# The gates of a hybrid mLSTM and attention layer as seven block products in place of eight, with an opening in another order

## What is computed

```python
mod = jax.nn.silu(c) @ w_ada[l] + b_ada[l]
shift, scale, gate = jnp.split(mod[:, None, :], 3, axis=-1)
h = rms_norm(x, g_norm[l]) * (1.0 + scale) + shift
proj = h @ w_in[l]
xa, va, oa, za, ia, fa, qa, ka, vat, zb, ga, gb = jnp.split(proj, split_at, axis=-1)
...
y_m = (h_m * jax.nn.silu(za)) @ w_out_mlstm[l]
...
y_a = (o_a * jax.nn.silu(zb)) @ w_out_attn[l]
merged = jax.nn.sigmoid(ga) * y_m + jax.nn.sigmoid(gb) * y_a
x = x + gate * (merged @ w_out[l])
return rms_norm(x, g_final)
```

## Time and profile before

| | us |
|---|---|
| median of 3 runs | 1460.41 |
| lowest, highest | 1460.26, 1461.08 |
| the profiled execution, its own time | 1462.57 |
| its span, first to last instruction | 1460.7 |
| TensorE busy | 1423.8 (97%) |
| VectorE busy | 764.3 (52%) |
| ScalarE busy | 485.3 (33%) |
| GpSimd busy | 368.1 (25%) |

### The profile page before, as it was taken

One profiled execution on the slowest core, in us unless ns is written; L12 is line 12 of the kernel. 1 busy time (PEld: TensorE's weight loads), 2 busy tenths in 40 slices (PEclk: granted clock), 3 DMA queues, 4 the chain that ended last, 5 costly groups with the idle time before them and its releaser, 6 DMA issues.

```text
span 1460.7 us, 18452 instructions
## 1 busy us (share of the span) xinstructions
PE 1423.8 (97%) x7465; PEld 1224.1 (84%) x7465; DVE 764.3 (52%) x1308; ACT 485.3 (33%) x859; POOL 368.1 (25%) x188
## 2 busy tenths in 40 slices
PE   3999999999999999999999999999999999999997
PEld 3698888889888888988888898888888888888885
DVE  6777566447466745635574554557373111112565
ACT  5666223443422353342335334323441000001122
POOL 3022111123111112211111221111154333443541
PEclk8999999999999999999999999999999999999998
DMA  6511111041221114211111421011172212124543
GB/s 258 186 58 53 39 35 39 30 145 60 100 65 45 44 36 150 83 31 43 30 29 30 145 73 44 30 30 43 31 279 82 65 65 66 65 65 152 155 135 111
DMA packets 51965, 117.79 MB, mean 81 GB/s; under 512 B 20769, under 2 KB 20897, under 8 KB 51877
## 3 DMA queue, kind: packets, MB, share of 16 engines
q1 hardware_dynamic: 47928, 104.01, 21.7%
q10 hardware_dynamic: 2832, 8.53, 1.9%
q0 software_dynamic: 1120, 4.06, 1.0%
HBM read 101.16 MB, written 15.43 MB: 80 GB/s over the span
## 4 chain that ended last, share of the span: by engine, by line
PE 92%; DVE 4%; DMA 3%; ACT 1%; issue 0%; SPq 0%; DVEq 0%; ACTq 0%
PE banks L464 26%; PE banks L463 26%; PE banks L462 26%; PE banks L747 2%; PE banks L737 2%; DMA x_rows<-in_x 2%; PE banks L698 2%; PE banks L704 2%; DVE y L1623 1%; PE banks L756 1%; PE banks L685 1%; PE banks L696 1%; PE banks L448 1%; PE banks L449 1%; PE banks L453 1%; PE banks L725 1%
## 5 line engine op out<-in xcount | busy, mean ns | idle before, releaser
L462 PE MATMUL banks<-h_hi,whi 128*128 128x512 f32 x1120 | 446.0, 398 | 0.0
L464 PE MATMUL banks<-h_hi,wlo 128*128 128x512 f32 x1120 | 437.4, 391 | 0.0
L463 PE MATMUL banks<-h_lo,whi 128*128 128x512 f32 x1120 | 436.5, 390 | 0.0
L602 POOL TENSOR_TENSOR wlo<-wraw,whi 128x1024 fp32r<-128x1024 f32 x75 | 192.0, 2560 | 842.4 <-ACT whi L827 842.4
L464 PEld LDWEIGHTS banks<-h_hi,wlo 128*128 128x128 f32 x1120 | 210.2, 188 | 44.6
L463 PEld LDWEIGHTS banks<-h_lo,whi 128*128 128x128 f32 x1120 | 210.6, 188 | 41.6
L462 PEld LDWEIGHTS banks<-h_hi,whi 128*128 128x128 f32 x1120 | 210.5, 188 | 41.1
L462 PE MATMUL banks<-whi,h_hi 128*128 128x256 f32 x480 | 135.8, 283 | 0.0
L464 PE MATMUL banks<-whi,h_lo 128*128 128x256 f32 x480 | 135.8, 283 | 0.0
L463 PE MATMUL banks<-wlo,h_hi 128*128 128x256 f32 x480 | 135.8, 283 | 0.0
L1471 DVE TENSOR_TENSOR num<-qa,banks 128x512 f32<-128x512 f32 x16 | 11.0, 688 | 184.6 <-PE banks L464 175.6
(11 more groups left out here) (271 smaller groups left out, 2248.0 us busy)
## 6 DMA issues: line engine op xcount, KB each, us to landing
wraw<-in_w_all SPq DMA_DIRECT2D x100, 512.0 KB, 3.5
s_wada<-in_w_ada_cols SPq DMA_DIRECT2D x16, 512.0 KB, 5.2
raw_lo<-in_x SPq DMA_DIRECT2D x8, 512.0 KB, 9.1
qm<-group_weights SPq DMA_DIRECT2D x8, 512.0 KB, 6.4
mlstm_branch<-xc SPq DMA_DIRECT2D x8, 512.0 KB, 8.7
part<-in_w_ada_gate SPq DMA_DIRECT2D x16, 256.0 KB, 3.4
b_raw<-mlstm_branch SPq DMA_DIRECT2D x8, 512.0 KB, 6.7
merged<-num ACTq DMA_DIRECT2D x8, 512.0 KB, 2.6
```

The source lines that it names most:

```text
L462: t_.matmul(out, w_hi, x_hi, start=first, stop=False)
L463: t_.matmul(out, w_hi, x_lo, start=False, stop=False)
L464: return t_.matmul(out, w_lo, x_hi, start=False, stop=last)
L602: nc.gpsimd.tensor_tensor(wlo[:, hi, :], wraw[:, q % 2, :], whi[:, hi, :].bitcast(F32), ALU.subtract).then_inc(w_split, 1)
```

## The change

**The gates.** The first pair of chunks (ga and gb of tile 0) is made as before, with the right half of the tokens first. The pairs 1 to 7 are made by seven products of blocks in place of eight. The weights of a pair are four quarters (ga or gb, first or second four row tiles) and h is four blocks (first or second four row tiles, left or right 512 tokens). Products 1 and 2 and 3 take a block of h as it is; products 5, 6, 7 and 4 take the sums t1, t2, t3 and t4 of blocks. Each product is 4 row tiles x 3 passes x 512 tokens. VectorE makes t1 ahead of `weigh_groups` of the last head, and t2, t3, t4 at the start of `merge`, in two pieces each of 128 x 1024; ScalarE copies their high parts and VectorE subtracts for the low parts. t3 is written over the h blocks that only the first pair reads. For each pair GpSimd makes four sums of quarters (`combine`, one of them in the new buffer `w_sum`) and seven low parts (`low`); ScalarE makes the seven high parts, in four places that go round (`weight_slot`). The results are put together by one copy on ScalarE (`keep_first`) and seven adds on VectorE (`plus`), each of one SBUF and one PSUM input, and the sigmoids are taken in place in SBUF and kept for all eight tiles.

**The order around them.** `merge_groups` of the last head moves behind the adds of pair 1. All branch products come after all gates. um and ua are loaded and split as the last pair ends, and w_out while the branches run, in rooms of their own. The softmax's exp of the last head (`group_exp`) is issued after the sigmoid of zb.

**The opening.** The first weight chunk is loaded ahead of x. VectorE squares tiles 0, 1, 6 and 7. GpSimd splits the second chunk only once the fifth tile is scaled. ScalarE keeps three transposed tiles before the second root.

**The closing.** TensorE waits for all three row vectors (48) in place of the gate's alone. Semaphores are merged in several places, and one counter of VectorE's steps serves all stages.

```diff
-BY_DVE = 2
+BY_DVE = (0, 1, 6, 7)
+BY_ACT = tuple(t for t in range(NCH) if t not in BY_DVE)
...
+        T["first_weights"](sp, 0)
         for t in range(NCH):
-            if t == NCH // 2:
-                T["first_weights"](sp, 0)
             sp.dma_start(x_raw[:, t, :], a["x"][t * P:(t + 1) * P, :]).then_inc(tile_in[t], 16)
...
         weights(0)
+        pool.wait_ge(x_norm, NCH // 2 + 1)
         weights(1)
...
+        A(xs[:, 2, 7:8], one[:], ACT.Abs_reciprocal_sqrt).then_inc(c_sig, 1)
+        act.wait_ge(c_sig, 3)
+        act.dma_start(m["szb"][0:ROPE, :].bitcast(I32), a["positions"].partition_broadcast(ROPE)).then_inc(pos_in, 16)
+        for t in BY_ACT:
             square(t)
-        root(0)
-        for t in range(NCH // 2, NCH - 1):
-            square(t)
-        keep_turned(0)
-        square(NCH - 1)
-        root(1)
-        act.dma_start(m["szb"][0:ROPE, :].bitcast(I32), a["positions"].partition_broadcast(ROPE)).then_inc(pos_in, 16)
-        for t in range(1, NCH):
+            if t == NCH // 2 - 1:
+                root(0)
+        for t in range(NCH):
+            if t == NCH // 2 - 1:
+                root(1)
             keep_turned(t)
...
+        for b in range(2):
+            for t in BY_DVE:
+                if t // 4 == b:
+                    square(t)
+            normalise(b)
...
             silu_za(1)
+            if i == HEADS - 1:
+                for q in range(2):
+                    ks = slice(2 * q, 2 * q + 2)
+                    t1 = T["sums"][1][2][:, ks, :]
+                    step(v.tensor_tensor(t1, h_hi[:, ks, HALF:].bitcast(F32), h_hi[:, ks, 0:HALF].bitcast(F32), ALU.subtract))
+                    step(v.tensor_tensor(t1, t1, h_lo[:, ks, HALF:].bitcast(F32), ALU.add))
+                    v.tensor_tensor(t1, t1, h_lo[:, ks, 0:HALF].bitcast(F32), ALU.subtract).then_inc(T["t_raw"], 1)
             weigh_groups()
             silu_zb()
-        merge_groups(HEADS - 1)
+        T["shared"]["merge_groups"] = merge_groups
...
+def products_of(p):
+
+    return (1, 5, 6, 2, 7, 4, 3) if p == 1 else (5, 4, 6, 7, 1, 3, 2) if p == KT - 1 else (5, 1, 2, 4, 6, 7, 3)
...
+    factors = {1: (h_hi[:, 0:KH, LEFT], h_lo[:, 0:KH, LEFT]), 2: (h_hi[:, KH:, LEFT], h_lo[:, KH:, LEFT]),
+               3: (h_hi[:, KH:, RIGHT], h_lo[:, KH:, RIGHT]), 4: (t4_hi[:], t4_lo[:]), 5: (t1_hi[:], t1_lo[:]),
+               6: (t2_hi[:], t2_lo[:]), 7: (t3_hi, t3_lo)}
+    sum_of = {5: 0, 6: 1, 7: 2, 4: 3}
+    quarter = {(r, c): raw[:, r, c * HALF:(c + 1) * HALF] for r in range(2) for c in range(2)}
+    spare = lambda p: mg if p == KT - 1 else sig[KT - 1][:, 1]
+    sums_of_weights = lambda p: {5: x_sum[:], 6: x_sum[:], 3: x_sum[:], 7: quarter[1, 0]} if p == 1 else \
+        {5: x_sum[:], 6: spare(p)[:, LEFT], 3: spare(p)[:, RIGHT], 7: x_sum[:]}
+    plain = {1: quarter[0, 0], 2: quarter[0, 1], 4: quarter[1, 1]}
+    source = lambda p, j: plain[j] if j in plain else sums_of_weights(p)[j]
+    made = lambda p, j: 4 * (p - 1) + ((5, 7, 6, 3) if p == 1 else (5, 6, 3, 7)).index(j) + 1
...
+        def load_pair(p):
+            for c in range(2):
+                sp.wait_ge(s_split, 1 + max(at_product(p - 1, j) for j in ((1, 2), (4, 7) if p == 2 else (4, 5))[c]))
+                sp.dma_start(raw[:, c, :], a["w_all"][Q0 + 2 * p + c]).then_inc(w_in[c], 16)
...
+        load_pair(2)
+        load_pair(3)
+        sp.wait_ge(T["ua_done"], HEADS + 1)
+        sp.dma_start(ua_d[HEADS - 1], T["mixing"]["szb"][:]).then_inc(ua_out, 16)
+        for p in range(4, KT):
+            load_pair(p)
...
+            if k % KH == 0:
+                sp.wait_ge(gprod, 1 + at_product(KT - 1, (5, 6)[k // KH]))
+            sp.dma_start(b_raw[k], um_d[k // 2, k % 2]).then_inc(tile_in[k], 16)
...
+        add, sub = ALU.add, ALU.subtract
+
+        def combine(out, x, y, op):
+            nc.gpsimd.tensor_tensor(out, x, y, op).then_inc(s_added, 1)
...
+            part = sums_of_weights(p)
+            if p > 1:
+                pool.wait_ge(s_split, PRODUCTS * (p - 1))
+            combine(part[5], quarter[1, 0], quarter[1, 1], add)
+            if p == 1:
+                pool.wait_ge(s_added, made(p, 5))
+                combine(part[7], quarter[0, 0], quarter[1, 0], sub)
+                low(1)
+                low(5)
+                after(5)
+                combine(part[6], part[5], quarter[0, 0], sub)
+                low(6)
+                after(6)
+                combine(part[3], quarter[0, 1], part[6], sub)
+                for j in (2, 7, 4, 3):
+                    low(j)
+            else:
+                low(5)
+                combine(part[6], part[5], quarter[0, 0], sub)
+                pool.wait_ge(s_added, made(p, 6))
+                combine(part[3], quarter[0, 1], part[6], sub)
+                after(5)
+                pool.wait_ge(s_added, made(p, 3))
+                combine(part[7], quarter[0, 0], quarter[1, 0], sub)
+                for j in products_of(p)[1:]:
+                    low(j)
+
+        for r in range(2 * KT):
+            n, to = width(r), (r + 1) % 2
+            pool.wait_ge(bw_high, r + 1)
+            nc.gpsimd.tensor_tensor(wlo[:, to, 0:n], raw[:, to, 0:n], whi[:, to, 0:n].bitcast(F32), sub).then_inc(bw_split, 1)
...
+        def product(p, j):
+            o = at_product(p, j)
+            bank_free(o)
+            to = bank(p, j)
+            pe.wait_ge(s_split, o + 1)
+            if p == 1 and j in sum_of:
+                pe.wait_ge(t_lo_done, 2 * sum_of[j] + 2)
+            hi, lo = factors[j]
+            at = weight_slot(o)
+            for k in range(KH):
+                cols = slice(k * P, (k + 1) * P)
+                mm = three_pass(t_, to, whi4[:, at, cols], wlo4[:, at, cols], hi[:, k, :], lo[:, k, :],
+                                k == 0, k == KH - 1)
+            mm.then_inc(gprod, 1)
...
+        for h in (1, 0):
             for j in range(2):
...
+                first_pair(j, h)
+        for p in range(1, KT):
+            for j in products_of(p):
+                product(p, j)
+        branch(um_at(0), 0, 0, KT, 0)
+        branch(um_at(1), 1, 0, KT, 0)
+        branch(ua_at(0), 0, KT, HEADS, 2)
+        branch(ua_at(1), 1, KT, HEADS, 2)
+        for m in range(2, KT):
+            branch(um_at(m), m, 0, KT, 0)
+            branch(ua_at(m), m, KT, HEADS, 2)
...
+        sum_high(1, t1_hi, t1_raw)
+        first_sigmoid(0, 1)
+        sum_high(2, t2_hi, t2_raw)
+        first_sigmoid(1, 1)
+        first_sigmoid(0, 0)
+        weight_high(1, 1)
+        weight_high(1, 5)
+        first_sigmoid(1, 0)
+        weight_high(1, 6)
+        weight_high(1, 2)
+        sum_high(3, t3_hi, t3_raw)
+        order_ = [(p, j) for p in range(1, KT) for j in products_of(p)]
+        for o in range(PRODUCTS * (KT - 2)):
+            p, j = order_[o]
+            if j == 1:
+                keep_first(p)
+            if o + 4 < len(order_) - 3:
+                weight_high(*order_[o + 4])
+            if o == 2:
+                sum_high(4, t4_hi, t4_raw)
+            if p > 1 and j == products_of(p)[1]:
+                sigmoids(p - 1)
...
+        weight_high(KT - 1, 1)
+        branch_high(0)
+        for k in range(2):
+            split_high(k)
+        weight_high(KT - 1, 3)
+        for k in range(2, 4):
+            split_high(k)
+        keep_first(KT - 1)
+        weight_high(KT - 1, 2)
+        for k in range(4, KT):
+            split_high(k)
+        branch_high(1)
+        sigmoids(KT - 1)
+        for k in range(KT, KB):
+            split_high(k)
+        branch_high(2)
...
+        def sum_raw(out, parts):
+
+            for q in range(2):
+                ks = slice(2 * q, 2 * q + 2)
+                t = out[:, ks, :]
+                (x, y, op), rest = parts[0], parts[1:]
+                ins = v.tensor_tensor(t, x[:, ks, :], y[:, ks, :], op)
+                for y, op in rest:
+                    step(ins)
+                    ins = v.tensor_tensor(t, t, y[:, ks, :], op)
+                ins.then_inc(t_raw, 1)
+
+        def sum_low(j, hi, lo, raw_):
+            for q in range(2):
+                ks = slice(2 * q, 2 * q + 2)
+                dve.wait_ge(t_hi_done, 2 * j - 2 + q + 1)
+                v.tensor_tensor(lo[:, ks, :], raw_[:, ks, :], f(hi[:, ks, :]), sub).then_inc(t_lo_done, 1)
+
+        def plus(p, name, out, x, j):
+
+            dve.wait_ge(gprod, 1 + at_product(p, j))
+            dve.wait_ge(part_added, added_part(p, name) - 1)
+            v.tensor_tensor(out, x, bank(p, j), add).then_inc(part_added, 1)
...
+        def merge_tile(m):
+
+            b0 = 4 * (m % 2)
+            if m == 0:
+                dve.wait_ge(s_split, PRODUCTS * (KT - 1))
+                dve.wait_ge(sig_done, 4 * KT)
...
+        dve.wait_ge(T["zb_done"], HEADS)
+        sum_raw(t2_raw, [(f(h_hi[:, KH:, RIGHT]), t1_raw, sub), (f(h_lo[:, KH:, RIGHT]), add)])
+        sum_low(1, t1_hi, t1_lo, t1_raw)
+        sum_low(2, t2_hi, t2_lo, t2_raw)
```

(40 more changed lines are left out.)

510 lines of the change are left out of this document (305 added, 205 removed).

## The result

The changed kernel takes **1468.68 us** (median of 5 runs, 1467.71 to 1469.03), the kernel before beside it 1460.41 (1459.85 to 1462.24). The ratio is 1.0053, 95% interval 1.0041 to 1.0064: slower by 6.0 to 9.4 us. I had forecast 1463.4 with a range up to 1468.0, so the time lies 0.7 us above the range. The kernel before has times of two kinds in the record of the first four experiments: 13 of its 23 executions took 1459.7 to 1461.3 us with a mean granted clock of 0.995 to 0.997, and ten took 1462.1 to 1463.1, nine of them with 0.992 or 0.993, as in the profiled execution (1462.57 us, 0.992).

What follows compares the result with a forecast made beforehand. PE, busy 97% of 1460.7 us, was taken to bound the kernel. Terms -19.0 - 1.2 + 0.4 + 19.1 + 2.6 + 1.1 = +3.0 us on the median 1460.41 gave 1463.4 us, eight-in-ten range 1446 to 1468.

Steps and rivals of the forecast that it cites:

- Term 1: Gates: 84 of 768 matmuls removed at 0.2267 us each, -19.0 us, all on PE.
- the 1405 that was named as a sign: Whole kernel, page of after: PE busy near 1405 us if the removal of matmuls holds.
- Term 2: Opening: Newton ends five us earlier, but blocked scalings and modulation sums leave -1.2 us, bounds -5.2 and 0.
- Term 3: First pair of gates, right half first: ScalarE's copy of its bank comes between, +0.4 us.
- Term 4: First new pair: VectorE's sums of h alternate with GpSimd; PE stalls 17.3 us, then half clock; +19.1 us.
- Later pairs: Gate pairs after the first new one: GpSimd's 14.3 us fit in PE's 19.0, costed at nothing.
- the third rival: Second new pair: GpSimd's low parts alternate with the merging and fall behind, +2 to +5 us more, 1467 us; chance 0.12.
- The prediction's own sign: Forecast is wrong if PE's waits in the first new pair sum under 8 us, or waits appear in later pairs.
- Term 5: Last pair and branches: two products wait 0.4 to 0.9 us each, um tiles 0 to 2; +2.6 us, bounds 0 and 5.
- Term 6: Closing: PE waits for all three rows, the last being gf, +1.1 us, bounds 0 and 1.5.
- The first rival: First new pair: sums of h hardly meet GpSimd, stall 3 to 7 us, total -12.2, 1448 us; chance 0.25.
- The second: Opening: gains its five us if modulation sums don't block on GpSimd, total about -0.8, 1459.6 us; no separate chance.

Runs made afterwards that it cites:

- e8: The changed kernel with ScalarE's second root ahead of the second to fourth copies of turned tiles: 1465.51 us, ratio 1.0029.
- e1: The kernel before with the changed kernel's new opening alone: 1462.63 us, ratio 1.0003.
- e5: The changed kernel with five useless matmuls between TensorE's last transposes and its first product: 1466.54 us, ratio 1.0035.
- e2: The changed kernel with GpSimd's low parts of the first new pair's weights covering 8 of 512 columns: 1461.71 us, ratio 1.0000.
- e9: e7 with the last szb sent after the fourth pair's weights and the last pair's first five sums one um split earlier: 1456.99 us, ratio 0.9968.
- e6: The changed kernel with merging after the second new pair, um low parts used for both token halves, and gate's own semaphore: 1472.21 us, ratio 1.0075.
- e11: The kernel before, with eight products, given the opening of e10: 1458.45 us, ratio 0.9976.
- e10: e9 with the opening's two edits, those of e5 and e8: 1453.80 us, ratio 0.9945.
- e7: The changed kernel with the edits of e4 and e6, and the first half of t3's sums in VectorE's wait before t4: 1466.88 us, ratio 1.0039.
- e4: The changed kernel with t4 formed from unsplit t2, ahead of t3, and first new pair's products in order 1, 5, 2, 6, 3, 4, 7: 1465.55 us.
- e12: e10 with twenty useless matmuls in the stall before the first new pair's fourth product: 1454.20 us, ratio 0.9956.

## Why the prediction missed

The mechanism that decides, VectorE's sums alternating with GpSimd and giving back what the removed matmuls save, was right, and the time was missed by 5.3 us. The steps that failed are these: the half clock behind the stalls was booked for one product (1.8 us, it took 3.9); the last pair and the branches were put at 2.6 and cost 4.7; the opening was put at -1.2 and gave nothing; the later pairs were costed at nothing and cost 1.0. Stalls in the first pair that were 4.3 us shorter than summed hid part of that. The last 1.9 us lie in the base that the sum was laid on.

**Term 1** was right to the record: 84 matmuls, 19.0 us. PE's busy time fell by 11.6 us to 1412.2, not to the 1405 that was named as a sign; a matmul's record is longer at half clock (0.63 us in place of 0.39), and there are more of these in after.

**Term 2, the opening: wrong.** The Newton steps took 0.16 us each, and the scaled tiles (6.47 us for four in place of 2.74) and the first two modulation sums (2.06 in place of 1.28) were blocked, as said. But the chain ended at 25.3 us, not at 24.0: VectorE waited 2.15 us for ScalarE's second root, longer than the term allows for; with the root early (e8) that wait is 0.27 us. So h_hi came at 36.30 (forecast 35.8 to 35.9, 37.57 before). The larger step that failed is "-1.7 us; PE rests longer before it and may run longer at half clock, so I take -1.2": between the two traces the half clock takes all of it. e1 gives 0.4 us slower within 1.3; e5 shows that the clock alone is worth up to 3 us there.

**Term 3** was right in kind: a wait of 0.34 us stands there, and the first gate product comes 0.2 us later behind the opening than before, where 0.4 were forecast.

**Term 4, the sums of h: mechanism right, sizes off both ways.** VectorE's chain decides, alternation with GpSimd is its price (e2), it gives back nearly all of term 1. The last low part ended at 1106.5, forecast 1109.5: it began at 1065.5 instead of 1066.4, and GpSimd's instructions cost it 1.0 us each instead of 1.2. That makes 3.0 us of the 4.3 by which the stalls, 13.0, fall short of 17.3; the rest is the half clock of product 7, 1.4 us, which lies ahead of the last stall and shortens it. The half clock was booked for product 4 alone, 1.8 us; it took 2.5 there and 1.4 in product 7. The term came to 16.9 instead of 19.1.

**Later pairs: wrong by 1.0.** I had priced the merging at nothing for PE, with the low parts at 3.3 us as a rival's mechanism. They took 2.2 to 2.6 and one stall of 1.0 us came: the third rival's mechanism at less than half its lowest price (2 to 5 us). The prediction's own sign, that it is wrong if waits appear in the later pairs, is met.

**Term 5, the last pair and the branches: 4.7 against 2.6, with the half clock the largest miss upward.** The low part of product 2 cost 1.0, where 0.4 to 0.9 for each of two products was said. The wait for the last um tiles was named with 0 to 2 us and took 2.2, for tiles 5 to 7. What was not named is that VectorE's splits of um stand in one line with the five sums of the last pair, for which the first branch product waited 1.5 us (PE's timeline of after; the profile calls that one "issue", and it went in e9, which makes those sums one split earlier):

```profile
1232.70 0.47 PE L486 MATMUL banks<-um_hi_a,whi 128*128 128x512 f32 x1 [1.35 <-issue]
...
1237.12 0.50 PE L486 MATMUL banks<-um_hi_b,whi 128*128 128x512 f32 x1 [0.78 <-DVE um_lo L1778]
```

e6 removed the waits for um and e9 the other as well, by order alone.

**Term 6** was right, 1.2 us for gf; 0.3 more came in the tail behind PE's last matmul.

**The sum's base.** The terms were made against a trace whose execution was 2.2 us above its median, and laid on the median. That is what the comparison wants, if the other kernel's profile is as far above its own median; it was only 0.35 above. The difference is 1.9 us, and with the terms' 3.4 us it makes the 5.3 between 1463.4 and 1468.7. Where the 1.9 us lie is not shown, but the opening is the likely place. Behind the row of the first low parts the three traces with eight products take the same time, 1416.5 us in before, 1416.8 in e1 and 1416.6 in e11. If that holds for an execution of before near its median, its row stood near 42 us, an estimate from these spans, and the new opening is then not worth 0.0 but costs 1 to 2 us. The medians of e1 and before, 1462.63 and 1460.80, say the same; the ratio, 0.9 us faster to 1.8 slower, allows it. My upper end, 1468, had no room for two misses at once.

The first rival, sums that hardly meet GpSimd, is excluded by e2 and by the rows of after themselves. Its sum has 1.5 us where term 5 stands with 2.6, and gives no reason; with 2.6 it would be 1449.3 and not 1448. The second, the opening's five us, is excluded by e1.

## What to carry to other kernels

When PE is at 97% and work is taken off it, count what the other engines must now do in one line before a deadline, stall by stall, and price every instruction of VectorE with two SBUF inputs at its own time plus what each GpSimd instruction that it meets costs it (here 1.0 us for one of 512 columns). Look for order before arithmetic: here moved sums, a queue entry, a loop order and a semaphore of its own turned +0.53% into -0.32%, and the only operations removed are two of VectorE's 24 instructions. Ask of a gain how much needed the new products: by e11, 0.24 of e10's 0.55% did not. Of each move, follow what its result leaves by: in e6 a store that waited for a late instruction held the weight loads issued behind it on the same engine.

## What the runs showed that I had not expected

Behind the stall of 4.05 us in after the first matmuls start 0.23 to 0.31 us apart and only then 0.43: the granted clock fell when TensorE was at work again. The rests of 4 to 8 us before products of the first pair had 6 to 14 matmuls at 0.43 us behind them, 1.3 to 2.9 us lost each. The rests of 2.6 us in e10 and 2.8 in e7 cost 1.6, as did one of 2.9 in e4's second pair; the one of 2.4 in e4's first pair and the one of 1.7 in e9 cost nothing. Useless work in a gap of 4.7 us gained 2 to 3 us in the opening, where PE was the bound again at once, and nothing in e12, where another engine was. And with the same opening its end wandered between 42.7 and 44.2 us, so one pair of traces can't tell a term of 1 us there.
